# Banded attention with row-half scores, divided probabilities and channel-major outputs

## The reference, cut to what matters

```python
def one_block(i):
    ...
    s = jnp.einsum('blkgd,bjkd->bkglj', qb, kb).astype(f32) + alibi
    s = jnp.where(valid, s, NEG_INF)
    m = jnp.maximum(jnp.max(s, axis=-1, keepdims=True), sink_l)
    p = jnp.exp(s - m)
    denom = jnp.sum(p, axis=-1, keepdims=True) + jnp.exp(sink_l - m)
    return jnp.einsum('bkglj,bjkd->blkgd', (p / denom).astype(vb.dtype), vb)
```

## Time and profile before

| what | value |
|---|---|
| median of 3 runs | 4013.04 us (4008.65 to 4015.49) |
| profiled execution | 4011.73 us, its span 4009.9 us |
| mean granted TensorE clock | 0.882 of full speed |
| PE busy | 3258.2 us, 81% |
| DVE busy | 2176.4 us, 54% |
| ACT busy | 1322.4 us, 33% |
| POOL busy | 413.2 us, 10% |
| attention stage, first bias add to last copy | 1702.3 to 1891.4 us |

### The profile page before, as it was taken

One profiled execution on the slowest core, in us unless ns is written; L12 is line 12 of the kernel. 1 busy time (PEld: TensorE's weight loads), 2 busy tenths in 40 slices (PEclk: granted clock), 3 DMA queues, 4 the chain that ended last, 5 costly groups with the idle time before them and its releaser, 6 DMA issues. The chain is left out here.

```text
span 4009.9 us, 59061 instructions
## 1 busy us (share of the span) xinstructions
PE 3258.2 (81%) x24837; PEld 2539.2 (63%) x24837; DVE 2176.4 (54%) x2625; ACT 1322.4 (33%) x1761; POOL 413.2 (10%) x273
## 2 busy tenths in 40 slices
PE   5699956599998996977877676967699982999995
PEld 1478654488886875755465463836566672888884
DVE  6622345456666334154374765747511146889885
ACT  1321233311111223133232332423311130777774
POOL 0200012300000011100020211212000000122210
PEclk7699878699999997988988787978799985999997
DMA  9131103111111322101101010010311232999996
GB/s 332 40 92 42 27 0 111 68 53 47 47 52 60 124 86 89 35 1 43 33 3 62 2 46 18 4 61 3 97 48 37 89 121 100 360 396 396 396 396 218
DMA packets 219885, 424.38 MB, mean 106 GB/s; under 512 B 12992, under 2 KB 122514, under 8 KB 219410
## 3 DMA queue, kind: packets, MB, share of 16 engines
q1 hardware_dynamic: 212306, 394.75, 27.5%
q0 software_dynamic: 4608, 16.78, 1.6%
q10 hardware_dynamic: 2753, 9.66, 0.6%
HBM read 387.61 MB, written 33.55 MB: 105 GB/s over the span
## 5 line engine op out<-in xcount | busy, mean ns | idle before, releaser
L213 DVE TENSOR_TENSOR w_exp_low<-w_exp,w_exp_high 128x2048 fp32r<-128x2048 f32 x192 | 438.0, 2291 | 55.4 <-ACT w_exp_high L208 55.4
L208 ACT ACTIVATE w_exp_high<-w_exp 128x2048 fp32r<-128x2048 f32 x192 | 368.0, 1920 | 124.8 <-PE psum L221 124.8
L219 PE MATMUL psum<-ffn_high,w_high 128*128 128x512 f32 x704 | 274.7, 390 | 9.0 <-DVE w_low L213 9.0
L220 PE MATMUL psum<-ffn_low,w_high 128*128 128x512 f32 x704 | 274.6, 390 | 0.0
L221 PE MATMUL psum<-ffn_high,w_low 128*128 128x512 f32 x704 | 274.4, 390 | 0.0
L1375 DVE SCALAR_TENSOR_TENSOR ffn_hidden<-u_padded,param_columns,ffn_hidden 128x1024 f32 (+1 forms) x176 | 226.2, 1285 | 23.8 <-DVE ffn_hidden L1371 0.2
L219 PE MATMUL psum<-w_exp_high,x_turned_high 128*128 128x512 f32 x512 | 203.5, 397 | 7.0 <-DVE w_exp_low L213 7.0
L1879 PE MATMUL psum<-mixers_hT,w_rkv 128*128 128x512 f32 x384 | 177.3, 624 | 37.8 <-DMA w_rkv<-in_w_in 37.8
L221 PE MATMUL psum<-w_exp_high,x_turned_low 128*128 128x512 f32 x512 | 200.8, 392 | 0.0
L220 PE MATMUL psum<-w_exp_low,x_turned_high 128*128 128x512 f32 x512 | 200.5, 392 | 0.0
L2314 DVE COPY inverse<-psum 64x512 f32<-64x512 f32 x192 | 121.8, 637 | 76.1 <-PE psum L2149 50.4
(11 more groups left out here) (439 smaller groups left out, 7936.0 us busy)
## 6 DMA issues: line engine op xcount, KB each, us to landing
w_exp<-in_exp_w_gate SPq DMA_DIRECT2D x32, 2048.0 KB, 12.5
w_exp<-in_exp_w_up SPq DMA_DIRECT2D x32, 2048.0 KB, 11.6
w_exp<-in_exp_w_down SPq DMA_DIRECT2D x32, 2048.0 KB, 14.2
ada_weights<-in_w_ada SPq DMA_DIRECT2D x12, 2048.0 KB, 14.6
w_raw<-in_w_up SPq DMA_DIRECT2D x44, 512.0 KB, 3.7
ffn_down_ring<-in_w_down SPq DMA_DIRECT2D x44, 512.0 KB, 3.5
mix_out_ring<-in_w_out SPq DMA_DIRECT2D x32, 512.0 KB, 3.5
mixers_hT<-hidden SPq DMA_DIRECT2D x4, 4096.0 KB, 13.1
```

Of the source, the lines that this page charges most:

```text
L208: return nc.scalar.activation(out, src, ACT.Copy, scale=scale)
L213: return nc.vector.tensor_tensor(out, src, high.bitcast(F32), ALU.subtract)
L219: nc.tensor.matmul(out, left[0], right[0], start=start, stop=False)
L220: nc.tensor.matmul(out, left[0], right[1], start=False, stop=False)
```

## The change

The stage is rewritten for the same 16 units:

- Scores read the queries where they lie. Each matmul uses one half of the partitions (64 rows of the array) for queries and keys; heads alternate between the halves. `q_padded` and POOL's copies are gone.
- DVE's division of the outputs is gone. Instead the probabilities are divided while they are rows: after the reciprocal, ACT scales heads 0 and 1 and POOL multiplies heads 2 and 3, a 128 x 768 operation.
- PE turns all twelve blocks of a unit in one piece, into banks 4 to 6, and ACT alone copies them out, 128 x 1536 in one operation.
- Outputs have the values as weights (64 columns; key head 0 in the left column half of the array, key head 1 in the right) and the turned probabilities of four heads as 512 moving columns: six matmuls for two units. They come out channel-major in bank 7, so that nothing is turned again.
- Scores and statistics have three slots.
- The channels of `att_out_cm` stand in another order, so the merge stage loads `w_proj_attn` in two transfers of 64 partitions, of half the bytes each, where one was.

```diff
@@ -1520,196 +1520,170 @@
     nc, dram, ps = core.nc, core.dram, core.psum
-    H, SP = 4, 3 * P
+    H, SP, SLOTS = 4, 3 * P, 3
     bias = core.at("alibi", 139, [P, AH, SP])
-    qs = core.at("q_padded", 151, [P, 2, 4, P])
-    sc = core.at("scores_sb", 155, [P, 2, H, SP])
-    pT = core.at("probs_turned", 28, [P, H, 3, P])
-    y = core.at("att_out", 34, [P, 2, 512])
-    sink = core.at("sink", 38, [P, AH])
-    stat = core.at("softmax_stat", 38.25, [P, 2, 6, H])
+    sc = core.at("scores_sb", 151, [P, SLOTS, H, SP])
+    pT = core.at("probs_turned", 28, [P, 2, 3, H * P])
+    sink = core.at("sink", 40, [P, AH])
+    stat = core.at("softmax_stat", 40.25, [P, SLOTS, 6, H])
...
+    NU = 2 * TT
     with Stage(core, "att") as s:
...
-        @s.b.gpsimd
-        def _(pool):
-            nc.gpsimd.memset(qs[:], 0.0).then_inc(zeroed, 1)
...
-                ins.then_inc(q_staged, 1)
         @s.b.tensor
         def _(pe):
             def scores(u):
                 i, g = divmod(u, 2)
-                pe.wait_ge(q_staged, u + 1)
                 if u:
                     pe.wait_ge(s_added, u)
                 for h in range(H):
-                    ins = nc.tensor.matmul(ps[:, h, 0:SP], qs[:, g, h], core.kd[:, g, i * P:i * P + SP],
-                                           start=True, stop=True)
+                    a = slice(64 * (h % 2), 64 * (h % 2) + 64)
+                    ins = nc.tensor.matmul(ps[:, h, 0:SP], core.q[a, 2 * g + h // 2, i * P:(i + 1) * P],
+                                           core.kd[a, g, i * P:i * P + SP], start=True, stop=True)
                 ins.then_inc(s_mm, 1)
-            def outputs(u):
-                i, g = divmod(u, 2)
-                pe.wait_ge(exp_done, u + 1)
...
-                    ins.then_inc(turned, 1)
+            def turn(u):
+                pe.wait_ge(act_scaled, u + 1)
+                pe.wait_ge(pool_scaled, u + 1)
                 if u:
-                    pe.wait_ge(y_done, u)
-                for h in range(H):
-                    pe.wait_ge(pT_done, 4 * u + h + 1)
...
-                pe.wait_ge(y_done, 2 * i + 2)
+                    pe.wait_ge(pT_done, u)
+                for b in range(3):
+                    for h in range(H):
+                        ins = nc.tensor.transpose(ps[:, 4 + b, h * P:(h + 1) * P], sc[:, u % SLOTS, h, b * P:(b + 1) * P],
+                                                  core.mask(M_ID))
+                ins.then_inc(turned, 1)
+            def outputs(i):
+                pe.wait_ge(pT_done, 2 * i + 2)
                 if i:
                     pe.wait_ge(yT_out, i)
-                for c in range(4):
-                    ins = nc.tensor.transpose(ps[:, 7, c * P:(c + 1) * P], y[:, i % 2, c * P:(c + 1) * P],
-                                              core.mask(M_ID))
-                ins.then_inc(y_turned, 1)
-            pe.wait_ge(zeroed, 1)
+                for b in range(3):
+                    for g in range(2):
+                        a = slice(64 * g, 64 * g + 64)
+                        ins = nc.tensor.matmul(ps[a, 7, :], core.av[:, i + b, g * ADH:(g + 1) * ADH], pT[:, g, b],
+                                               start=(b == 0), stop=(b == 2))
+                ins.then_inc(y_mm, 1)
             scores(0)
             scores(1)
             for u in range(NU):
                 if u + 2 < NU:
                     scores(u + 2)
                 if u >= 2 and u % 2 == 0:
-                    turn_outputs(u // 2 - 1)
-                outputs(u)
-            turn_outputs(TT - 1)
+                    outputs(u // 2 - 1)
+                turn(u)
+            outputs(TT - 1)
         @s.b.scalar
         def _(act):
-            def front(u):
-                g = u % 2
+            def exponentials(u):
+                j = u % SLOTS
                 act.wait_ge(sink_sub, u + 1)
                 for h in range(H):
-                    nc.scalar.activation(sc[:, g, h], sc[:, g, h], ACT.Exp, bias=stat[:, g, NM, h:h + 1],
-                                         accum_out=stat[:, g, RS, h:h + 1])
-                nc.scalar.activation(stat[:, g, ES], stat[:, g, SM], ACT.Exp).then_inc(exp_done, 1)
...
-                                         ).then_inc(pT_done, 1)
+                    nc.scalar.activation(sc[:, j, h], sc[:, j, h], ACT.Exp, bias=stat[:, j, NM, h:h + 1],
+                                         accum_out=stat[:, j, RS, h:h + 1])
+                nc.scalar.activation(stat[:, j, ES], stat[:, j, SM], ACT.Exp).then_inc(exp_done, 1)
+            def scale(u):
+                j = u % SLOTS
+                act.wait_ge(den_done, u + 1)
+                for h in range(2):
+                    ins = nc.scalar.activation(sc[:, j, h], sc[:, j, h], ACT.Copy, scale=stat[:, j, DEN, h:h + 1])
+                ins.then_inc(act_scaled, 1)
+            def take_turned(u):
+                act.wait_ge(turned, u + 1)
+                if u >= 2:
+                    act.wait_ge(y_mm, u // 2)
+                nc.scalar.activation(pT[:, u % 2].rearrange("p b n -> p (b n)"),
+                                     ps[:, 4:7, :].rearrange("p b n -> p (b n)"), ACT.Copy).then_inc(pT_done, 1)
             def take_outputs(i):
-                act.wait_ge(y_turned, i + 1)
+                act.wait_ge(y_mm, i + 1)
                 nc.scalar.activation(yT[:, :, i * P:(i + 1) * P], ps[:, 7, :].rearrange("p (c t) -> p c t", c=4),
                                      ACT.Copy).then_inc(yT_out, 1)
-            front(0)
-            front(1)
             for u in range(NU):
-                if u >= 2 and u % 2 == 0:
-                    take_outputs(u // 2 - 1)
-                back(u)
-                if u + 2 < NU:
-                    front(u + 2)
+                exponentials(u)
+                if u:
+                    take_turned(u - 1)
+                if u >= 3 and u % 2:
+                    take_outputs((u - 3) // 2)
+                scale(u)
+            take_turned(NU - 1)
             take_outputs(TT - 1)
+        @s.b.gpsimd
+        def _(pool):
+            for u in range(NU):
+                j = u % SLOTS
+                pool.wait_ge(den_done, u + 1)
+                nc.gpsimd.tensor_tensor(sc[:, j, 2:4], sc[:, j, 2:4],
+                                        stat[:, j, DEN, 2:4].unsqueeze(2).to_broadcast([P, 2, SP]), ALU.mult
+                                        ).then_inc(pool_scaled, 1)
         @s.b.vector
         def _(dve):
-            def front(u):
+            def maximum(u):
                 nonlocal ordered
                 i, g = divmod(u, 2)
+                j = u % SLOTS
                 dve.wait_ge(s_mm, u + 1)
-                if u >= 2:
-                    dve.wait_ge(turned, 4 * (u - 1))
-                nc.vector.tensor_tensor(sc[:, g], ps[:, 0:4, 0:SP], bias[:, 4 * g:4 * g + 4, :], ALU.add
+                if u >= SLOTS:
+                    dve.wait_ge(turned, u - SLOTS + 1)
+                nc.vector.tensor_tensor(sc[:, j], ps[:, 0:4, 0:SP], bias[:, 4 * g:4 * g + 4, :], ALU.add
                                         ).then_inc(s_added, 1)
                 dve.wait_ge(s_added, u + 1)
...
-                nc.vector.reduce_max(stat[:, g, MX], sc[:, g], axis=AX).then_inc(order, 1)
-                dve.wait_ge(order, ordered + 1)
-                nc.vector.tensor_tensor(stat[:, g, MX], stat[:, g, MX], sink[:, 4 * g:4 * g + 4], ALU.max
+                nc.vector.reduce_max(stat[:, j, MX], sc[:, j], axis=AX).then_inc(order, 1)
+                ordered += 1
+            def with_sink(u):
+                nonlocal ordered
+                g, j = u % 2, u % SLOTS
+                dve.wait_ge(order, ordered)
+                nc.vector.tensor_tensor(stat[:, j, MX], stat[:, j, MX], sink[:, 4 * g:4 * g + 4], ALU.max
                                         ).then_inc(order, 1)
-                ordered += 2
-                dve.wait_ge(order, ordered)
-                nc.vector.tensor_scalar(stat[:, g, NM], stat[:, g, MX], -1.0, None, ALU.mult)
...
                 ordered += 1
                 dve.wait_ge(order, ordered)
+                nc.vector.tensor_scalar(stat[:, j, NM], stat[:, j, MX], -1.0, None, ALU.mult)
+                nc.vector.tensor_tensor(stat[:, j, SM], sink[:, 4 * g:4 * g + 4], stat[:, j, MX], ALU.subtract
+                                        ).then_inc(sink_sub, 1)
+            def denominator(u):
+                nonlocal ordered
+                j = u % SLOTS
+                dve.wait_ge(exp_done, u + 1)
+                nc.vector.tensor_tensor(stat[:, j, DEN], stat[:, j, RS], stat[:, j, ES], ALU.add).then_inc(order, 1)
+                ordered += 1
+                dve.wait_ge(order, ordered)
+                nc.vector.reciprocal(stat[:, j, DEN], stat[:, j, DEN]).then_inc(den_done, 1)
-            front(0)
-            front(1)
             for u in range(NU):
-                back(u)
-                if u + 2 < NU:
-                    front(u + 2)
```

(14 more changed lines are left out.)

62 lines of the change are left out of this document (5 added, 57 removed).

## The result

| | before | after |
|---|---|---|
| median (range) of 4 runs each, us | 4014.26 (4008.65 to 4017.12) | 3919.98 (3913.96 to 3924.63) |
| profiled execution, its span, us | 4011.73, 4009.9 | 3924.63, 3922.8 |
| attention, from the issue of its bias table to the next stage's first load, us | 197.3 | 109.5 |

The changed kernel takes 0.9772 of the time (95% interval 0.975 to 0.9794), 94 us less by the medians. The profiled execution of the changed kernel is the slowest of its four, so the two profiled spans differ by 87.1 us only, and the attention stage by 87.7; nothing measurable happened elsewhere. In the merge stage the matmuls that use the projections' weights span 269.4 us in both traces, from 2899.9 to 3169.3 before and from 2809.9 to 3079.3 after, so the extra transfers cost nothing.

What follows compares the result with a forecast made beforehand. Bound: a ring of waits in attention, 11.98 us a unit. Stage end: 1700.7 + 4.5 + 89.0 (15 x 5.93) + 1.6 + 13 + 5 = 1813.8 against 1891.4, -77.6: forecast 3935, main case 3927 to 3943, range 3918 to 3960.

Steps and rivals of the forecast that it cites:

- the old ring: Attention stage before: add, scores, turn, outputs and division wait for one another, 11.98 us a turn, 16 turns.
- rival D: POOL's multiply with repeated operand is far slower; at 10 us for 768 elements the kernel takes 4048; chance 0.02.
- rival A: POOL's use of the shared port costs DVE nothing; ACT's 5.1 us a unit sets the pace, 3922; chance 0.17.
- the longest list sets the pace: Attention stage after: each engine runs its own list, and the longest, DVE's 5.93 us a unit, decides.
- Start, +6.3 us after the issue: Stage's start: bias table issued at 1694.4, first add at 1700.7 instead of 1702.3, so -1.6 us.
- DVE's list, 5.93: DVE's work per unit: 4.22 us, plus 1.71 from small operations caught by POOL's multiply.
- Lateness, +5 us: Scores coming late when PE's lower clock falls on outputs and turn: +5 us over the stage, bounds 0 and 12.
- Memsets, 1.6 apart from the pace: Three more memsets in the attention stage, adding 1.6 us beside the 15 units' pace.
- End, 13 us: After the last subtraction: exponentials, copies, scaling, turn and outputs take 12 to 14.5 us, taken as 13.
- PE, 9.0 of 11.9 for two units: PE's list for two units: scores 2.8, turn 2.6, outputs 2.6, changes and tails 1.0; nothing late at upper clock.
- rival C: Array halves do not run side by side at 384 and 512 columns: 3950 to 3967; chance 0.06.
- Rival B: PE at the lower clock almost throughout, making it the bound at 8.2 us a unit: 3964; chance 0.18.

Runs made afterwards that it cites:

- e1: Changed kernel with DVE's three small operations ahead of the previous unit's denominator, so that none meets POOL's multiply: 3922.5 us, ratio 0.9769.
- e10: Changed kernel with outputs issued by unit, one column half at a time, two units late and ahead of the turn: 3915.5 us, ratio 0.975.
- e11: Changed kernel with POOL dividing all four heads, DVE's small operations first, and outputs issued by unit, two units late: 3918.3 us, ratio 0.9765.
- e6: Kernel before the change with only the scores by row halves and without POOL's padding: 4010.6 us, ratio 0.999.
- e8: Changed kernel with POOL dividing all heads, DVE's small operations first, a third turned-rows buffer, outputs behind the next turn: 3947.8 us, ratio 0.9833.
- e9: Changed kernel with DVE's small operations first, a third turned-rows buffer, outputs behind the next turn and their copy a unit later: 3936.8 us, ratio 0.9811.
- e12: Changed kernel with POOL dividing all four heads, DVE's small operations first, and DVE instead of ACT copying the outputs: 3917.5 us, ratio 0.974.
- e5: Changed kernel with two slots instead of three for scores and statistics: 3962.5 us, ratio 0.9869.
- e2: Changed kernel without POOL's multiply, ACT scaling all four heads: 3937.3 us; stage 14.1 us longer, where the theory of an ACT-PE ring over two units said 15.
- e3: Changed kernel with outputs issued one column half after the other instead of alternating: 3929.4 us, ratio 0.9786.
- e4: Changed kernel with the scores' heads in the order 0, 2, 1, 3: 3922.1 us, ratio 0.9768.

## Why the prediction was right, and where it wasn't

The direction and the mechanism of the gain were right: the old ring fell apart, and the adds stand half as far apart, 5.53 us on average between the first and the last where they stood 11.16. (The 11.98 that I read was one of the longer units; only rival D's sum used it.) The time, 3920, is inside the range but below the likeliest case's own 3927 to 3943: the room left for rival A held it, and not A's reason. The step that failed is **"the longest list sets the pace"**, with its term of 5.93 us a unit, where the adds were 5.53 apart on average and the ring held 5.56.

- **Start, +6.3 us after the issue**: 6.33. Right.
- **DVE's list, 5.93**: measured 5.34. POOL's multiply took 1.50 where a row gave 1.8, so the reciprocal stands 1.70 ahead of the next add, not 2.17; the reduce took 0.11 less to its successor. The block itself was as told: the subtraction ends with POOL. The Trainium skill (SBUF — State Buffer, "Who interferes with whom") has it that an operation with two SBUF inputs is locked out for the other's whole instruction, and that whoever issues first holds the pair; the trace agrees, 1.43 for the subtraction, 0.17 for a negation that starts with POOL's multiply.
- **"The longest list sets the pace"**: it didn't. The ring that ends in ACT's wait for the turn took 11.11 for two units, and without the block (e1) 11.12. I had listed just this as what would make the forecast wrong, PE's turn behind the outputs. It released ACT, though, not the adds. ACT's list was 10.3 of the 11.1 us, close to the 5.1 a unit that I had given it: what I missed is that a wait of 0.85 on the way, on an engine that is 92% busy, has no slack to come out of.
- **Lateness, +5 us**: the term was for turns of the clock, and its value measured is about 0: the granted clock was 0.91, and 15 intervals sum to 82.9 us, where 15 x 5.56 are 83.4.
- **Memsets, 1.6 apart from the pace**: they show in the adds of the second and the fifteenth unit, 6.01 and 6.00 to the next, and were made up for by shorter intervals at the start (4.79, 5.34, 5.33).
- **End, 13 us**: 14.0.
- Sum of these: from the first add to the last subtraction I had 100.1 us (4.5 + 89.0 + 1.6 + 5); it took 88.95 (1702.81 to 1791.76). Of the 11.15 less, 5.6 are the pace, 5 the lateness. With the end's 1.0 more, the saving is 10.1 larger than the 77.6 forecast: 87.7.
- **PE, 9.0 of 11.9 for two units**: scores 1.5 x 2, turn 1.5 x 2, outputs 2.75: 8.8 of 11.1. Pairs ran side by side, as rival C denied; e10 shows it from the other side.
- **Rival B** (PE at the lower level almost throughout): didn't happen, 0.91. The Trainium skill's sentence on transposes and the clock (TensorE: Matmul & The Clock Gate, Part 4: PE-mode transpose) made it likelier than it was; here turns are a third of PE's work, and in e11, with PE at its fullest, the clock was 0.96 in the same stretch.
- **Rival A** (port costs nothing): half its reason, and its time, 3922, by luck. The block exists, 1.3 us of each unit, and costs nothing, because DVE would wait for scores instead. But A's pace was 5.1, and 5.56 came, 5.6 us less over the stage and not 12.5; most of the difference was made up by the lateness of 5 that A kept and that didn't occur.
- **What bounds the kernel before**: I drew the ring through the scores. In e6, with row halves, they were not on it. That didn't hurt the forecast, since the change takes the whole ring apart, but a forecast for the row halves alone from that paragraph would have failed, as its expectation of 25 to 45 us did.

## What to carry to other kernels

When a ring of waits is taken apart, the longest list of one engine is only a lower bound: write down, for two units, every wait that crosses engines, and close the loops, above all through the engine with little slack. Moving work in one engine's order takes it out of one loop and puts it into another (e8, e9), and each fix is worth only the distance to the next loop (e10, e12). A buffer slot can be worth nearly half of a change (e5: 41 of 88 us, the clock that fell with it included), and an operation made shorter off the ring brought nothing (e6, at a lower clock). A run whose time fits a theory proves little until its waits are read: e2's 14 us looked like R's 15 and had another cause.

## What the runs showed of the hardware that was not expected

- Two column halves at the price of one: 12 records of 128x512 in pairs took 2.79 us, 6 of one half alone 2.79 as well (e10). Issued half after half in one go, 12 took 3.70, with the middle eight in pairs (e3). For row halves the order of heads made no difference (1.57 against 1.56, e4).
- POOL's multiply with a repeated operand: 1.50 us for 128x768 and 2.75 for 128x1536; by an estimate from these two, 1.63 ns an element and 0.25 us besides.
- An operation of four elements with one SBUF input can be held for the whole of POOL's multiply, or not at all, and the recorded starts don't tell which. Timeline of the changed kernel:
```profile
1739.17 1.47 POOL L1632 TENSOR_TENSOR scores_sb<-scores_sb,softmax_stat 128x768 f32<-128x768 f32 x1 [3.83 <-DVE softmax_stat L1678]
1739.18 1.48 DVE L1667 TENSOR_SCALAR softmax_stat<-softmax_stat 128x4 f32<-128x4 f32 x1
...
1761.39 1.50 POOL L1632 TENSOR_TENSOR scores_sb<-scores_sb,softmax_stat 128x768 f32<-128x768 f32 x1 [3.84 <-DVE softmax_stat L1678]
1761.40 0.17 DVE L1667 TENSOR_SCALAR softmax_stat<-softmax_stat 128x4 f32<-128x4 f32 x1
```
  Both times the negation starts 0.01 us behind the multiply; once it takes 1.48 us, once 0.17. It was caught in 2 of 16 units, where the multiply took 1.47; in 13 others, where the multiply took 1.50, the subtraction was caught instead.
- Less work for PE and a lower granted clock together, 0.71 against 0.85, with the same busy time (e6). Variants of the changed stage with the same matmuls, differing in order, slots and waits alone, had from 0.78 (e5, e8) to 0.94 (e1) from first to last add.
